# One fused decoder step: six landing buffers for gathered expert rows, and one quarter of the query weights kept resident

## What is computed

```python
def peer(h, wq, subkeys, pu, pv):
    ...
        q = (xb @ wq).reshape(blk, PEER_HEADS, 2, PEER_DK_HALF)
        s = jnp.einsum('thpc,hpnc->thpn', q, subkeys).astype(jnp.float32)
        sv, si = lax.top_k(s, PEER_TOPK)
        cand = (sv[:, :, 0, :, None] + sv[:, :, 1, None, :]).reshape(blk, PEER_HEADS, PEER_TOPK * PEER_TOPK)
        ...
        fv, fi = lax.top_k(cand, PEER_TOPK)
        eidx = jnp.take_along_axis(cidx, fi, axis=-1)
        gate = jax.nn.softmax(fv, axis=-1)
        act = jax.nn.gelu(jnp.einsum('thkd,td->thk', pu[eidx], xb).astype(jnp.float32), approximate=False) * gate
        return jnp.einsum('thk,thkd->td', act.astype(xb.dtype), pv[eidx])
```

## Time and profile before

| what | us |
|---|---|
| median of 3 runs (lowest, highest) | 2055.16 (2050.91, 2058.91) |
| the profiled execution | 2059.03 |
| its span, first to last instruction | 2057.2 |
| first gather issued | 597.6 |
| last gather issued | 2028.6 |
| PE busy | 1627.0 (79%) |
| DVE busy | 1353.0 (66%) |
| POOL busy | 815.4 (40%) |
| ACT busy | 668.3 (32%) |
| bytes moved by the core's DMA engines | 729.2 MB, 354 GB/s over the span |

### The profile page before, as it was taken

The page is one execution under the profiler, slowest core; times in us unless marked ns, Lnnn a source line. Parts: engine busy times, 40 slices in busy tenths (PEclk is TensorE's granted clock), DMA queues, the critical chain, the costliest instruction groups (busy, mean ns, idle before and its releaser), DMA issues.

```text
span 2057.2 us, 26082 instructions
## 1 busy us (share of the span) xinstructions
PE 1627.0 (79%) x8272; PEld 866.1 (42%) x8272; DVE 1353.0 (66%) x3086; ACT 668.3 (32%) x1962; POOL 815.4 (40%) x604
## 2 busy tenths in 40 slices
PE   6999988887878896675789576659967778887776
PEld 4545446545655452343355233324533443332222
DVE  4245866654468876656887655687867668676754
ACT  2111222211124452323445333344533333442332
POOL 0188573223014453433444333444435334444441
PEclk9999999988998997989799889989988999999999
DMA  8378654986689999999999999999999999999996
GB/s 300 109 259 279 216 168 152 310 278 217 212 307 413 419 417 413 414 414 422 391 403 402 414 373 414 421 420 401 402 414 379 417 418 419 421 420 421 421 421 266
DMA packets 168937, 729.20 MB, mean 354 GB/s; under 512 B 17621, under 2 KB 18598, under 8 KB 102098
## 3 DMA queue, kind: packets, MB, share of 16 engines
q0 software_dynamic: 75024, 545.82, 64.5%
q1 hardware_dynamic: 93778, 181.73, 25.6%
HBM read 718.50 MB, written 9.09 MB: 354 GB/s over the span
## 4 chain that ended last, share of the span: by engine, by line
PE 38%; DMA 29%; DVE 15%; issue 6%; ACT 4%; SPq 4%; POOL 2%; another core or an unknown queue 0%; DVEq 0%; POOLq 0%; ACTq 0%
PE bank L486 37%; DMA R<-in_peer_uv,R 13%; DMA RING<-in_peer_uv,R 11%; DMA R<-in_w_out 4%; DVE RING L2218 4%; SPq L2472 3%; DVE R L2218 2%; ACT R L1378 1%; PE bank L493 1%; SPq L2531 1%; POOL MV L2382 1%; DMA R<-in_cache_v 1%; DMA RING<-in_w_mod 1%; DVE R L1964 1%; ACT R L1388 1%
## 5 line engine op out<-in xcount | busy, mean ns | idle before, releaser
L2458 POOL DMA_INDIRECT RING<-in_peer_uv,R x390 | 441.6, 1132 | 680.5 <-PE bank L486 556.2
L486 PE MATMUL bank<-RING,R 128*64 128x512 f32 (+2 forms) x1560 | 508.2, 658 | 212.5 <-ACT R L1378 202.6
L486 PE MATMUL bank<-R 128*128 128x128 f32 (+6 forms) x2184 | 395.0, 376 | 89.9 <-ACT R L1378 78.3
L2218 DVE SCALAR_TENSOR_TENSOR RING<-RING,MV 128x1024 f32<-128x1024 f32 x288 | 351.7, 1223 | 172.7 <-DMA RING<-in_peer_uv,R 162.5
L486 PEld LDWEIGHTS bank<-R 128*128 128x128 f32 (+3 forms) x2184 | 257.4, 185 | 256.7 <-issue 248.9
L486 PEld LDWEIGHTS bank<-RING,R 128*64 128x64 f32 (+2 forms) x1560 | 156.7, 158 | 463.8 <-issue 452.3
L1388 ACT ACTIVATE R<-R 128x2 f32<-128x2 f32 x256 | 51.9, 203 | 748.0 <-DVE RING L2218 598.3
L2458 POOL DMA_INDIRECT R<-in_peer_uv,R x130 | 152.3, 1171 | 227.8 <-PE bank L486 210.0
L2218 DVE SCALAR_TENSOR_TENSOR R<-R,MV 128x1024 f32<-128x1024 f32 x96 | 117.4, 1223 | 58.7 <-DMA R<-in_peer_uv,R 54.5
L2218 DVE SCALAR_TENSOR_TENSOR RING<-RING,R 128x1024 f32<-128x1024 f32 x96 | 117.4, 1223 | 58.1 <-DMA RING<-in_peer_uv,R 52.3
L486 PEld LDWEIGHTS bank<-HT,R 128*128 128x128 f32 x1024 | 122.3, 194 | 51.9 <-issue 51.9
(11 more groups left out here) (336 smaller groups left out, 1826.5 us busy)
## 6 DMA issues: line engine op xcount, KB each, us to landing
R<-in_peer_wq SPq DMA_DIRECT2D x16, 2048.0 KB
RING<-in_w_mod SPq DMA_DIRECT2D x12, 2048.0 KB, 8.1
MV<-in_cache_k SPq DMA_DIRECT2D x88, 256.0 KB, 3.7
R<-in_cache_v SPq DMA_DIRECT2D x84, 256.0 KB, 3.5
R<-in_w_out SPq DMA_DIRECT2D x6, 2048.0 KB
MV<-in_cache_v SPq DMA_DIRECT2D x44, 256.0 KB, 3.7
RING<-in_w_in SPq DMA_DIRECT2D x5, 2048.0 KB, 9.8
R<-in_cache_k SPq DMA_DIRECT2D x40, 256.0 KB, 3.6
```

Of the source, the lines that this page charges most:

```text
L486: i = nc.tensor.matmul(out, lhsT, rhs, start=start, stop=stop, **k)
L2218: V.scalar_tensor_tensor(u, u, 1.0, H2HIGH if s_ % 2 and n < PAIRED * PH else H2[n // PH % 2], ALU.mult, ALU.mult, accum_out=DOT[:, n % 4, ...
L2458: nc.gpsimd.indirect_dma_start(UV[g % UN], None, a["peer_uv"][0], bass.IndirectOffsetOnAxis(ap=idx, axis=0)).then_inc(S(f"uv_in{g % UN}"), 16)
```

## The change

The landing buffers become six, all in `RING`. The two pieces of `R1` and `R2` that are freed hold quarter 0 of `wq` (`WR`, four of the eight k-blocks in each). It is loaded once, ahead of the loop, and used by all four tiles. `w_parts` therefore has three parts for tile 0 and five for each later tile, and which of the two weight slots a part uses alternates from tile to tile. SyncE's list at the start of the loop is reordered.

```diff
@@ -195,7 +195,8 @@
-        UV = [part(FLAT, i * 2048, 2048) for i in range(6)] + [part(R1, 12288, 2048), part(R2, 8192, 2048)]
+        UV = [part(FLAT, i * 2048, 2048) for i in range(6)]
+        WR = [part(R1, 12288, 2048, k=4, n=512), part(R2, 8192, 2048, k=4, n=512)]
         UN = len(UV)
@@ -395,9 +396,9 @@
-        w_parts = [(0, "wq", c) for c in range(4)]
+        w_parts = [(0, "wq", c) for c in range(1, 4)]
         for tile in range(1, TILES):
-            w_parts += [(tile, "wo", c) for c in range(2)] + [(tile, "wq", c) for c in range(4)]
+            w_parts += [(tile, "wo", c) for c in range(2)] + [(tile, "wq", c) for c in range(1, 4)]
@@ -940,7 +941,8 @@
                 for k in ks:
-                    mm(b[:, 0:n], w[:, k, j * P:(j + 1) * P], HT[:, k, i * P:i * P + n], k == 0, k == KT - 1, full(job) if k == KT - 1 else None)
+                    wk = w[:, k, :] if c else WR[k // 4][:, k % 4, :]
+                    mm(b[:, 0:n], wk[:, j * P:(j + 1) * P], HT[:, k, i * P:i * P + n], k == 0, k == KT - 1, full(job) if k == KT - 1 else None)
@@ -979,7 +981,8 @@
-            w = w_slot(pe, 0, "wq", 0)
+            pe.wait_ge(S("wr_loaded"), 32)
+            w = None
@@ -1013,7 +1016,7 @@
-                    w = w_slot(pe, i, "wq", c) if j == q == 0 else W[w_parts.index((i, "wq", c)) % 2]
+                    w = None if c == 0 else w_slot(pe, i, "wq", c) if j == q == 0 else W[w_parts.index((i, "wq", c)) % 2]
@@ -2705,8 +2708,10 @@
             job_done(sp, ("dS", 0))
+            load(WR[1], wq[:, 4:8, 0:512], "wr_loaded")
+            job_done(sp, ("pt", 7))
+            load(WR[0], wq[:, 0:4, 0:512], "wr_loaded")
             weights_in(0)
-            job_done(sp, ("pt", 7))
             load(KN, a["peer_subkeys"][0].rearrange("h p n c -> n (h p) c"), "keys_in")
             weights_in(1)
@@ -2715,14 +2720,13 @@
-            for m in range(2, 4):
-                weights_in(m)
+            weights_in(2)
@@
-                elif kind == "wq" and j == 3 and q == 1:
+                elif kind == "wq" and c and j == 3 and q == 1:
```

## The result

The changed kernel takes 2142.88 us (median of 4 runs, 2132.86 to 2145.43) against 2057.03 us for the kernel before in the same set of runs. That is 86 us slower; the ratio of the runs is 1.0405, 95% interval 1.0376 to 1.0435. The forecast was 2084 us, with a range of 2041 to 2122. The sign was right; the forecast loss of 29 us was a third of the measured one. The profiled execution took 2132.86 us, 73.8 us more than that of before, so it lies at the fast end of its kernel.

A forecast was written before the change was run, and what follows sets the result against it. The prediction took DMA bytes to bound two thirds of the loop, with PE and DMA both near their bounds in the delta stage. Terms -15.2 + 6 + 2 + 6 + 30 = +29 gave 2084 us, range 2041 to 2122.

The forecast's parts named there:

- The start: Before the first gather: sub-keys queue behind 3.15 MB of `wq`, so PE starts 1.5 to 10.8 us late; +6 taken.
- The byte term: Weights stage: three quarters of `wq` not loaded again, 6.29 MB at 413 GB/s, all of it counting: -15.2 us.
- +30: Delta stage, 508 us: loss from two buffers fewer, between 0 and 116 us; a quarter of the upper bound taken.
- The step that failed: Shortest loop where no weights are under way: 7.30 us hold plus 7.14 us way, 14.4 us, fits six gathers' 15.0 us.
- Tile 3: Last tile, only gathers: six buffers fit with 1.4 us to spare; +2 us for places where DVE's top-k work intervenes.
- Weights stage: 595 us where weights load: bytes -15.2 us; two buffers fewer +6 us, 1.5 for each of PE's four `w_out` stands.
- Gathers that come later cost PE nothing: Delta stage, lower bound: hold over 7.30 us is only queue before a full PE and shrinks with later gathers; loss 0.
- The queue was not needed: Rival, chance 0.26: loop closes in 14.4 us everywhere and bytes decide; faster or the same, 2044 to 2055 us.
- Weights arrive sooner: Rival, chance 0.07: `w_out` arrives earlier with fewer gathers ahead, removing up to half of 34.6 us of stands; 2029 us.
- Held time stays: Rival, chance 0.10: delta-stage buffers stay held 11.72 us, costing all of 116 us; 2179 us, or 2120 with half.
- The rule of the skill: Gather way of 4.4 us: delta loop needs 11.7 to 16.1 us, six buffers suffice nearly everywhere, only -15 and +6 remain.

The follow-up runs named there:

- the one that waits six back: Kernel before, eight buffers and all weights loaded, but each gather waits for the value matmul six steps before it instead of eight: 2147.3 us.
- the one with the sub-keys first: Changed kernel with the sub-keys issued ahead of the half quarter and the quarter of `wq`: 2139.3 us.
- the constant in its place: Kernel before with six buffers, quarter 0 of `wq` not loaded for tiles 1 to 3, a constant block multiplied instead: 2135.8 us.
- the short loop: Changed kernel, value matmul with the identity instead of the diagonal of gates, waiting for the landing alone: 2056.4 us; with all quarters loaded 2068.5 us.

## Why the prediction was right in sign and wrong in size

**What was right.** The bound by bytes (two thirds of the loop), the loop as the thing to look at, and that its queue of 6 us is what two buffers take away. The start: "I take the middle: +6", measured +6.3, of which 5.5 are the order of loads and the rest was there before. The byte term: 15.2 us, measured 14 with eight buffers. That the delta stage carries most of the loss. The sign rests on the "+30", which the prediction calls a choice: without it its sum is -1, so the sign was in part luck.

**The step that failed** is the length that the loop needs. The prediction took a short way of a gather (7.14 us) and a short hold of a buffer (7.30) and said "with 7.14 it is 14.4, against 6 x 2.5 = 15.0. It fits with 0.6 to spare". The five-buffer kernel shows 16.7 to 16.9 us as the mean round in that part of the program and 15.7 in tile 3. I had added up two short pieces of different rounds and taken the sum for every round; they were not even the shortest, since later runs have ways down to 5.4 us. Of the 2.3 us between 14.4 and 16.7, the gather's way is 8.2 - 7.14 = 1.1. A reason lies in the rows: POOL issues two gathers 1.24 us apart when a pair is freed, and the second stands behind the first. The other 1.2 us are longer holds. With 16.7 instead of 14.4, six buffers give 2.78 us per gather where the DMA engines take 2.5, and a late round is not an exception: with five buffers 72% of the rounds in the delta stretches are longer than the 15.0 us that six gathers give.

The mean alone is not the whole of it. With eight buffers the delta stretches already take 2.74 us per gather (608.0 / 222), where PE is nearly full, and 2.78 would add only 9 us. Measured are 3.00. Rounds scatter, and a long one stops the transfers once no gather is left in the queue, while a short one can't make up for it. The prediction said so itself ("each such irregularity was covered by a queue of 6 us and will now find 1") and sized it with a quarter of its upper bound. That reading fits the rounds; no run changes the scatter and leaves the mean.

**Term by term.**

- *Tile 3*, "+2": measured +12.2, end included. Here the mean loop is enough: 15.7 / 6 = 2.62 us per gather against 340.2 / 135 = 2.52 before is +13. The prediction's own sign was met, a rate of 410 GB/s or less (405).
- *Weights stage*, -15.2 + 6 = -9: measured +0.7. It is the "+6" that was too small. At the stage's bounds the profiled executions of six-buffer kernels with all loads take 615.2 and 612.5 us there (buffers alone, and the one that waits six back), those without the reloads of quarter 0 take 601.8, 605.9 and 601.9 (the changed kernel, the one with the sub-keys first, and the constant in its place). So the bytes are still worth some 11 us, and the two buffers cost some 13 instead of 6. Whether "the whole of it counts" holds with six buffers these few executions can't say; the totals give 7 us with an error of the same size.
- *Delta stage*, "+30", called a choice and not a reading: measured +54.7. The bounds, 0 and 116, held. The quarter that I took did not; it was nearly half.
- *Gathers that come later cost PE nothing*: they cost it clock. On the page of after the mean granted clock is 0.901 against 0.921, and PE is busy for 1669 us instead of 1627 with the same matmuls. The rows of one place in the kernel after, delta stage of tile 1:

```profile
670.42 3.68 PE L487 MATMUL bank<-RING,R 128*64 128x512 f32 x8 [4.23 <-ACT R L1381]
...
674.34 0.94 POOL L2461 DMA_INDIRECT RING<-in_peer_uv,R  x1 [7.71 <-PE bank L487]
...
681.33 1.94 PE L487 MATMUL bank<-RING,R 128*64 128x512 f32 x8 [0.61 <-ACT R L1381]
```

and the granted clock there, by stretch as in the earlier trace rows:

```profile
671.00:672.00 1.00, 1.00 (x4) 0.27 (x2) 1.00 (x2) 0.00 (x0) 0.00 (x0) 0.50 0.98 401
```

After a stand of 4.23 us the granted clock was 0.50, the lower of the clock's two levels, and the same eight value matmuls took 3.68 us instead of 1.94, so that the two buffers were freed 1.7 us later. Whether that makes the next stand longer the rows don't show; the next ones are short. How much this adds on the whole shows in the value matmuls by form (busy us, mean ns, idle before), first before, then after, then five buffers:

```profile
L486 PE MATMUL bank<-RING,R 128*64 128x512 f32 x1152 | 316.4, 674 | 164.8 <-ACT R L1378 158.8 <-issue 6.0
...
L486 PE MATMUL bank<-R 128*64 128x512 f32 x384 | 105.9, 675 | 59.4 <-ACT R L1378 54.9 <-issue 4.5
```

```profile
L487 PE MATMUL bank<-RING,R 128*64 128x512 f32 x1536 | 448.6, 710 | 263.4 <-ACT R L1381 255.0 <-issue 8.1
```

```profile
L486 PE MATMUL bank<-RING,R 128*64 128x512 f32 x1536 | 489.9, 768 | 378.0 <-ACT R L1378 377.7
```

192 pairs took 422 us before and 449 after, 0.14 us more per pair, and 0.35 more with five buffers. That is small against a loop that is 1.7 us over the 15.0 that six gathers give it. What a slower clock does to PE's other work in the delta stage is not in this figure. It was read, not tested: no run here holds the clock fixed.

**The rivals.** "The queue was not needed" fell with the six-buffer run (2142.6). "Weights arrive sooner" is there in the trace (the stands for `w_out` fell from 34.6 to 20.7 us), too small to be seen in the total. "Held time stays", to which I gave 0.10 and 2179 us or half of it, 2120, was the nearest in number. Its mechanism doesn't hold: a buffer was held 11.72 us in the earlier trace rows, and with six buffers the mean in the delta stretches is 9.2.

**The rule of the skill.** The fit of the Trainium skill, page "DMA: Bandwidth & Descriptors", section "Anatomy of one DMA — SWDGE (gpsimd) path", of about 2.0 us and the bytes at 436 GB/s gives 4.4 us for 1 MiB (an estimate from that page). The gather's median here is 8.2 us even with five buffers, and the shortest 5.4. The trace doesn't agree, at least not for gathers of 8 KB rows with others under way; how long one takes by itself no run here shows.

## What to carry to other kernels

The number of landing buffers that a stream needs follows from the round of a buffer (hold and way, with the queue short) and the time that the bytes of one buffer take. The mean is only the lower end: here 16.5 / 2.5 = 6.6, and yet seven lose 16 us, because a third of the rounds are longer than seven gathers; six lose 88 and five 285. To get the rounds before a change, don't add short pieces of a trace in which the queue is long; take one buffer more away than you mean to, so that the loop binds nearly everywhere, and read the rounds off the issue times, mean and scatter. Before saving bytes at the price of buffers, ask whether the loop still closes with room to spare; if it doesn't, shorten the loop first.

## What the runs showed of the hardware

- A gather of 128 rows of 8 KB takes a median of 8.2 us from issue to landing when five are allowed out, 8.9 with six in the full loop and 11.2 with six in the short loop, where the DMA engines are full again.
- A plain load of 2 MiB takes 9.8 us where no gathers run and around 30 beside them, less with fewer gathers allowed out: the median for `w_out`, whose two loads are issued together, is 28.1 us with five buffers, 28.9 to 33.1 with six, 33.5 with seven, 34.5 with eight and a quarter left out. The kernel before shows one such wait on its chain, 28.39 us. With five buffers, then with eight:

```profile
R<-in_w_out SPq DMA_DIRECT2D x6, 2048.0 KB, 28.1
```

```profile
R<-in_w_out SPq DMA_DIRECT2D x6, 2048.0 KB, 34.5
```

- The DMA engines' busy share is a poor measure of a stream that runs dry: with five buffers tile 3 shows 0.92 at 338 GB/s, with eight 1.01 at 421.
- PE's granted clock was 0.921 with eight buffers, 0.901 with six and 0.873 with five, and with the same matmuls it was busy for 1627, 1669 and 1746 us.
